# Key norms by squares and summed products instead of by the gram's diagonal, and the decay made at the head pair's own slot

## The reference, cut to what matters

```python
q, k, v = jnp.split(silu(causal_depthwise_conv(proj[..., :3072], conv_w)), 3, axis=-1)
k = t * lax.rsqrt(jnp.sum(t * t, axis=-1, keepdims=True) + RMS_EPS)      # t = k, per head; q likewise
g = -jnp.exp(a_log) * softplus(a + dt_bias)
gc = jnp.cumsum(g in chunks of 64)
decay = jnp.exp(jnp.where(causal, gc[..., :, None] - gc[..., None, :], -jnp.inf))
lower = jnp.where(strict, (k_beta @ k.T) * decay, 0)                     # solved as (lower + eye) x = rhs
attn = (q @ k.T) * decay
# scan over the 8 chunks, state carried along
v_new = u_c - w_c @ state
o_c = q_c @ state + a_c @ v_new
state = state * g_last + k_c.T @ v_new
```

## Time and profile before

| | before |
|---|---|
| median of 3 runs | 1973.99 us (1973.04 to 1975.83) |
| the profiled execution | 1975.83 us, its span 1974.0 us |
| granted TensorE clock, mean | 0.998 |
| PE busy | 1942.9 us, 98% of the span |
| DVE busy | 1161.7 us, 59% |
| ACT busy | 828.9 us, 42% |
| POOL busy | 28.6 us, 1% |
| chain that ended last | PE 86%, DVE 7%, ACT 4%, issue 2% |

### The profile page before, as it was taken

One profiled execution on the slowest core, in us unless ns is written; L12 is line 12 of the kernel. 1 busy time (PEld: TensorE's weight loads), 2 busy tenths in 40 slices (PEclk: granted clock), 3 DMA queues, 4 the chain that ended last, 5 costly groups with the idle time before them and its releaser, 6 DMA issues.

```text
span 1974.0 us, 28498 instructions
## 1 busy us (share of the span) xinstructions
PE 1942.9 (98%) x11058; PEld 1592.2 (81%) x11058; DVE 1161.7 (59%) x1899; ACT 828.9 (42%) x1347; POOL 28.6 (1%) x32
## 2 busy tenths in 40 slices
PE   9999999999999999999999999999999899999998
PEld 7776788888888787888888888778878678888887
DVE  6556477634556766667543654878887656424533
ACT  5456554333334444454333333545564632212232
POOL 0111000000000000000000000100000000000000
PEclk9999999999999999999999999999999999999999
DMA  6222122233223111122223224111211122232221
GB/s 217 76 75 96 43 80 92 89 103 106 86 80 112 70 65 65 65 86 86 101 87 111 91 76 142 64 50 50 70 44 44 65 86 91 101 107 86 105 87 64
DMA packets 30795, 168.40 MB, mean 85 GB/s; under 512 B 6456, under 2 KB 6616, under 8 KB 14816
## 3 DMA queue, kind: packets, MB, share of 16 engines
q1 hardware_dynamic: 25872, 161.69, 23.4%
q10 hardware_dynamic: 4816, 5.22, 0.8%
HBM read 163.72 MB, written 2.13 MB: 84 GB/s over the span
## 4 chain that ended last, share of the span: by engine, by line
PE 86%; DVE 7%; ACT 4%; issue 2%; DMA 0%; SPq 0%; DVEq 0%; ACTq 0%
PE bank L509 25%; PE bank L511 24%; PE bank L510 24%; PE bank L1148 2%; PE bank L792 1%; ACT hH L1337 1%; DVE hL L2152 1%; PE bank L975 1%; ACT wH L1337 1%; DVE x L2148 1%; PE bank L815 1%; PE bank L999 1%; PE bank L804 1%; PE bank L1226 1%; PE bank L1208 1%
## 5 line engine op out<-in xcount | busy, mean ns | idle before, releaser
L509 PE MATMUL bank<-hH,wH 128*128 128x512 f32 x1368 | 550.5, 402 | 1.7 <-DVE hL L2114 1.7
L511 PE MATMUL bank<-hH,wL 128*128 128x512 f32 x1368 | 532.6, 389 | 0.0
L510 PE MATMUL bank<-hL,wH 128*128 128x512 f32 x1368 | 531.7, 389 | 0.0
L1337 ACT ACTIVATE wH<-raw 128x2048 fp32r<-128x2048 f32 (+3 forms) x199 | 294.2, 1489 | 119.2 <-PE bank L511 104.8
L509 PEld LDWEIGHTS bank<-hH,wH 128*128 128x128 f32 x1368 | 257.6, 188 | 60.4 <-issue 8.4
L511 PEld LDWEIGHTS bank<-hH,wL 128*128 128x128 f32 x1368 | 257.1, 188 | 54.6
L2066 DVE TENSOR_TENSOR wL<-raw,wH 128x2048 fp32r<-128x2048 f32 x96 | 219.7, 2289 | 134.6 <-ACT wH L1337 134.6
L510 PEld LDWEIGHTS bank<-hL,wH 128*128 128x128 f32 x1368 | 257.8, 188 | 48.0 <-issue 1.2
L509 PE MATMUL bank<-mH,wH 128*128 128x512 f32 (+1 forms) x610 | 232.8, 382 | 0.0
L511 PE MATMUL bank<-mH,wL 128*128 128x512 f32 (+1 forms) x610 | 232.6, 381 | 0.0
L510 PE MATMUL bank<-mL,wH 128*128 128x512 f32 (+1 forms) x610 | 232.6, 381 | 0.0
(11 more groups left out here) (354 smaller groups left out, 2796.1 us busy)
## 6 DMA issues: line engine op xcount, KB each, us to landing
raw<-in_ffn_up SPq DMA_DIRECT2D x44, 1024.0 KB, 4.8
raw<-in_mlp_up SPq DMA_DIRECT2D x16, 1024.0 KB, 4.7
raw<-in_mlp_down SPq DMA_DIRECT2D x16, 1024.0 KB, 4.8
raw<-in_ffn_down SPq DMA_DIRECT2D x16, 768.0 KB, 4.1
raw<-in_odd_in SPq DMA_DIRECT2D x12, 1024.0 KB, 4.7
raw<-in_dn_qkv SPq DMA_DIRECT2D x12, 1024.0 KB, 4.8
raw<-in_ffn_down SPq DMA_DIRECT2D x16, 640.0 KB, 3.9
raw<-in_even_in SPq DMA_DIRECT2D x7, 1024.0 KB, 5.1
```

What stands on the lines that cost most here:

```text
L509: mm(out, a, c, start=first, stop=False, skip_group_check=joined)
L510: mm(out, a, d, start=False, stop=False, skip_group_check=joined)
L511: return mm(out, b, c, start=False, stop=last, skip_group_check=joined)
L1337: return nc.scalar.activation(out, in_, func, **kw)
```

## The change

- `key_sums` on VectorE goes. For pairs 1 to 3 ScalarE squares the keys at slot 48p-14 and TensorE sums them at slot 48p-12 with `squares_summed` into bank 4; `key_norm` moves to slot 48p-11 (was 48p-8), `key_base` to 48p-11 (was 48p-7), `key_exponents` to 48p-9 (was 48p-6).
- the gram of keys by keys of pairs 1 to 3 moves from slot 48p-10 and bank 4 to slot 48p and bank 3, ahead of the gram with the queries.
- the decay's exponent and Exp of pairs 1 to 3 move from slots 48p-6 and 48p-5 to 48p and 48p+1; the block from `lt` to the first transpose moves from 48p+1 to 48p+2.
- two of the preloads of the LOG_EXP set go, at the softplus of the gates and at `key_norm`.
- the turned gate rows are 64 instead of 32 (the cumulated gates and their Exps), turned at slot 10 (was 7), in bank 6 (was 7), and copied at VectorE's slot 7 (was 8); they are stored at ScalarE's slot 13 (was 10).
- `o_squared` waits for other events, since the buffer `sq` is used in another order.

```diff
-        rowsG, gl, gcB = sb("rowsG", [32, P]), sb("gl", [P, H, 8]), sb("gcB", [P, SEQ])
+        rowsG, gl, gcB = sb("rowsG", [64, P]), sb("gl", [P, H, 8]), sb("gcB", [P, SEQ])
-        key_size, tot = tok[:, 0, :], tok[:, 3, :]
+        key_size, gc_egc, tot = tok[:, 0, :], tok[:, 1:3, :].rearrange("p a b -> p (a b)"), tok[:, 3, :]
@@ TensorE
-                if t == 7:
-                    pe.wait_ge(*at("dn.gc_copied"))
-                    pe.wait_ge(*at("dn.lnss0"))
-                    nc.tensor.transpose(bank[7][0:32, 0:P], tok[:, 1, :], ident).then_inc(*tick("dn_gate_pe", "dn.rows_turned"))
+                if t == 10:
+                    pe.wait_ge(*at("dn.egc"))
+                    nc.tensor.transpose(bank[6][0:64, P:2 * P], gc_egc, ident).then_inc(*tick("dn_gate_pe", "dn.rows_turned"))
             def key_scalars(p, t):
-                if p and t == 38:
+                if p and t == 36:
                     pe.wait_ge(*at(f"dn.bv{p - 1}.1"))
-                    pe.wait_ge(*at(f"dn.silu{6 * p + 1}"))
-                    grams(p, 4, 0, f"dn.kk{p}")
+                    squares_summed("k", p, bank[4][:, 0:8])
...
-                                mm(bank[2][part(e), chunk(n)], ident[0:32, n:n + 1].to_broadcast([32, 64]), rowsG[:, part(e)],
+                                mm(bank[2][part(e), chunk(n)], ident[0:64, n:n + 1].to_broadcast([64, 64]), rowsG[0:64, part(e)],
...
-                        grams(p, 3, 0, f"dn.kk{p}")
                     else:
                         pe.wait_ge(*at(f"dn.y{p - 1}.5"))
+                    grams(p, 3, 0, f"dn.kk{p}")
+                    if p:
                         pe.wait_ge(*at(f"dn.silu{6 * p + 3}"))
                         grams(p, 2, 1, f"dn.qk{p}")
@@ ScalarE
-                a(lnss[:, p, :], lnss[:, p, :] if p else bank[7][:, 0:8], ACT.Ln, bias=eps)\
+                a(lnss[:, p, :], bank[4][:, 0:8] if p else bank[7][:, 0:8], ACT.Ln, bias=eps)\
...
                 a(gates_abs, gates_raw, ACT.Abs).then_inc(*tick("dn_gate_act", "dn.abs"))
-                nc.scalar.preload_act_table_set(LOG_EXP)
                 a(coef, v("a_log", 0, 8), ACT.Exp)
...
-                if t == (-5 if p else 1):
+                if t == 1:
                     act.wait_ge(*at(f"dn.din{p}"))
                     a(dec[:], dec[:], ACT.Exp).then_inc(*tick("dn_prep_act", f"dn.dec{p}"))
-                if t == 1:
                     squares_of("q", p, 1, f"dn.ksum{p}", *([f"dn.os{p - 2}.1"] if p >= 2 else []))
...
-                act.wait_ge(*at(f"dn.os2.{f}" if p == 3 else f"dn.qsum{p + 1}"))
+                act.wait_ge(*at(f"dn.os2.{f}" if p == 3 else f"dn.qsum{p + 1}" if f == 0 else f"dn.ksum{p + 2}" if p < 2 else "dn.qsum3"))
...
-                if t == 10:
+                if t == 13:
                     gate_rows_out()
...
-                    if t == 48 * p - 8:
-                        nc.scalar.preload_act_table_set(LOG_EXP)
+                    if t == 48 * p - 14:
+                        squares_of("k", p, 0, f"dn.qsum{p - 1}", *([f"dn.os{p - 2}.0"] if p >= 2 else []))
+                    if t == 48 * p - 11:
                         key_norm(p)
-                    if t == 48 * p - 6:
+                    if t == 48 * p - 9:
                         key_exponents(p)
@@ VectorE
-                if t == 8:
+                if t == 7:
                     dve.wait_ge(*at("dn.rows_turned"))
-                    nc.vector.tensor_copy(rowsG[:], bank[7][0:32, 0:P]).then_inc(*tick("dn_gate_dve", "dn.rows"))
-            def key_sums(p):
-                dve.wait_ge(*at(f"dn.kk{p}"))
-                dve.wait_ge(*at(f"dn.qsum{p - 1}"))
-                if p >= 2:
-                    dve.wait_ge(*at(f"dn.os{p - 2}.0"))
-                chain(tt(blocks(sq[:, 0, :]), blocks(bank[4][:]), over_chunks(eye), ALU.mult), "dn_scalar_dve", f"dn.diag{p}")
-                nc.vector.tensor_reduce(lnss[:, p, :], blocks(sq[:, 0, :]), AX.X, ALU.add).then_inc(*tick("dn_scalar_dve", f"dn.ksum{p}"))
+                    nc.vector.tensor_copy(rowsG[:], bank[6][0:64, P:2 * P]).then_inc(*tick("dn_gate_dve", "dn.rows"))
...
-                if t == (-6 if p else 0):
+                if t == 0:
                     dve.wait_ge(*at(f"dn.masked{p}" if p else "dn.spread0"))
...
-                if t == (1 if p else 2):
+                if t == 2:
                     dve.wait_ge(*at(f"dn.kk{p}"))
                     dve.wait_ge(*at(f"dn.dec{p}"))
-                    chain(tt(lt[:], bank[4 if p else 3][:], dec[:], ALU.mult), "dn_prep_dve", f"dn.lt{p}")
+                    chain(tt(lt[:], bank[3][:], dec[:], ALU.mult), "dn_prep_dve", f"dn.lt{p}")
...
-                    if t == 48 * p - 9:
-                        key_sums(p)
-                    if t == 48 * p - 7:
+                    if t == 48 * p - 11:
                         key_base(p)
```

More of the change, by code:

```diff
@@ L1877, in gate_rows_out @@
                 act.wait_ge(*at("dn.rows"))
-                act.dma_start(dram["gc_rows"], rowsG[:]).then_inc(*tick("dn_rows_stored", "dn.rows_stored", 16))
+                act.dma_start(dram["gc_rows"], rowsG[0:32, :]).then_inc(*tick("dn_rows_stored", "dn.rows_stored", 16))
             def gate_rows_in(p):
```

## The result

The changed kernel takes 1983.9 us (median of 6 runs, 1982.18 to 1985.61), the kernel before 1973.7 us beside it. The ratio is 1.0051, with a 95% interval from 1.0039 to 1.0063: 10 us slower, outside the 0.2% that a measurement of this kernel can tell. The profiled execution took 1984.93 us, its span 1983.1 us against 1974.0.

A forecast was written before the change was run, and what follows sets the result against it. TensorE, busy 98% of the span, was taken as the bound. Pairs 2.9 + 4.3 + 4.3 and gates -0.4 gave +11.1 us on a 1973.99 median: 1985.1 us, range 1977 to 1991.

The forecast's parts named there:

- The prep block: VectorE's block from lt to the first transpose, at slot 48p+2, delays the next solve: +2.0 us a pair.
- the bound of 2.8: Upper bound in us for the prep block's cost per pair, if all of it shows; lower bound 0.
- Rival C: The prep block hides, VectorE skipping ahead because TensorE is late too: +5.1 us, 1979.1; chance 0.10.
- The opening: Scan opening of pair 2 (pair 3 the same): write 1.5 us later, about 0.3 comes back, +1.2 at slot 96.
- The sums on TensorE: Key sums as 32 matmul records on TensorE for pairs 1 to 3, never hidden: 1.1 us each, 3.3 together.
- The table loads: ScalarE without the named set: ten more loads, 1.28 us each, costing only where TensorE waits; drain left out.
- rival A: One table set serves Ln and Exp, so the load at slot 48p-9 goes: +8.4 us, 1982.4; chance 0.14.
- Gates: First pair's gate rows turned at slot 10, copied earlier, one more load: -0.4 us, between -2 and +1.
- Rival B: Not slower: scalars are ready before the scan opens, idle 5.0 us goes, block fits: -2.1 us, 1971.9; chance 0.18.
- Rival D: Longer gaps bring half clock, one stretch behind each pair's opening, adding 5.1 us: 1990.2; chance 0.10.
- The signs: Profile after: solve waits about 10.8 us on VectorE, write 6 to 7 on ScalarE, ten loads, 96 records more.

The follow-up runs named there:

- experiment 1: The kernel before run again with no edit, against itself: 1974.19 against 1974.2 us, ratio 1.000.
- Experiment 4: The changed kernel with the decay's part undone (exponent at 48p-6, Exp at 48p-5, block at 48p+1): 1979.91 us, ratio 1.003 to the kernel before.
- experiment 3: The kernel before with the decay's part alone (exponent at slot 48p, Exp at 48p+1, block at 48p+2): 1991.7 us, ratio 1.0087.
- Experiment 8: The changed kernel with VectorE's block moved from slot 48p+2 to 48p+4, behind the right side, for pairs 1 to 3: 1987.38 us, ratio 1.0065 to the kernel before.
- experiment 7: The changed kernel with the sixteen products summing the keys' squares done twice in pairs 1 to 3: 1985.14 us, ratio 1.005 to the kernel before.
- Experiment 6: The changed kernel with the LOG_EXP set loaded by name again at the softplus and at slot 48p-11: 1981.21 us, ratio 1.0032 to the kernel before.
- experiment 9: The kernel before with key sums, Ln, Exps and decay spread over the scan's opening, behind the right side and vBlk: 1970.66 us, ratio 0.9985.
- experiments 1 to 4: The runs of experiment 1, of the gates' part alone on the kernel before (1972.76 us), of experiment 3 and of Experiment 4.

## Why the prediction was right

**The sum.** 1985.1 us was forecast and 1983.9 measured; in the profiled executions +11.1 and +9.1 us. The forecast's own mechanism is the one that the trace shows. Of its excess of 2.0 us the three pairs make 2.05 (0.66 + 0.71 + 0.68 less than worked out); what else moved (+0.96, -1.54 and +0.65 in the table) nearly cancels, and that is luck: none of the three was in the sum, and experiment 1 shows the first two without any change.

**The prep block, +2.0 a pair.** It measured 1.8 (5.67 against 3.86 us), in the order that was written down: state update, block, tap, right side. Experiment 4 gives 4.5 us for the three by the times and 5.3 by the traces. But experiment 3 corrects the reasoning: the bound of 2.8 ("all of it shows") was not the upper one, for ScalarE's Exp can start the block late, and the clock can fall on top. Rival C's argument, that the second gram gives VectorE 1.1 us, was dismissed for two reasons. The first, that VectorE waits for ScalarE's decay, is wrong for the changed kernel: its Exp ends at 1412.29, and the block starts at 1413.40, right behind the state update and output. The second, that the state update is queued first, holds: VectorE stood idle for 3.27 us ahead of it. Experiment 8 removes the thought that putting the block behind the right side would be enough.

**The opening, +1.2 at slot 96.** Measured +0.95 (solve of slot 96, 2.19 less 1.24). The steps came as worked out: 0.41 us of wait for the square (0.35 forecast), the first write 1.7 us later (1.45 forecast), the solve of slot 90 0.87 (1.2), the write of slot 92 1.15 (1.5) with a wait of 1.89, all counted from slot 84. The profile puts the solve's wait (0.69) down to ScalarE's read copy in pair 2 and to VectorE in pair 3: in pair 2 the copy ended at 1400.30 and the right side at 1400.29, TensorE going at 1400.54. The two end together, as close as the prediction had said.

**The sums on TensorE, "in full", 1.1 each.** One such group takes 1.03 us from start to start. "In full" was too strict: experiment 7 shows that in pair 2 a second group hides altogether, so that the opening there is set by ScalarE and VectorE; pair 3 has the same opening, but no undisturbed trace of it. In pair 1 all but the block came to 0.5 us (0.9 forecast). What the change costs by its sums alone was not separated.

**The table loads.** Ten more, as forecast. Experiment 6's trace puts four of them at 2.9 us, for which the working for rival A had 2.7 (1.06 in each of pairs 2 and 3 against 1.1, and 0.74 at the gates against 0.5). Rival A itself is out: the Trainium skill (ScalarE: Activation LUTs, Table sets: the hidden batching unit) has Ln and Exp share one load. Experiment 6's trace agrees, where the set is named; the changed kernel's, without the name, shows two (1395.18 and 1397.71). Nor does it show the drain of about 1.38 us that the Trainium skill (ScalarE: Activation LUTs, What ACT_TABLE_LOAD costs) adds to a load: the read copy of 1399.57 ends at 1400.30, the load runs from 1400.33 to 1401.61, and the SiLU starts at 1401.62. So leaving the drain out of the sum was right.

**Gates, -0.4.** Measured -0.42, with the waits 0.2, 0.31 and 0.79 where 0.5, 0.8 and 0.55 were worked out. The sum was better than its parts.

**Rival B, not slower.** It was to be decided by whether ScalarE ends its Exps before TensorE's read of slot 88. It did not: the read started at 1397.86, the Exps ended at 1399.67, in the time of before at 1398.4, where 1398.6 was worked out. B's mechanism is real, but not in this change: by experiment 9 some 3 us of the opening's waits go when the work is put behind vBlk. The change put it ahead, with two more loads and a square.

**Rival D.** No half-clock stretch stands behind an opening in the changed kernel's trace. But the rival is not out for every execution: the traces of experiments 7 and 8 have one in the opening of pair 3 and of pair 2. The changed kernel's own six times went from 1982.18 us at a mean clock of 1.000 to 1985.61 at 0.997. The one at the gates of the earlier trace rows is absent too, which gives its trace 1.5 us; I had not counted on that, and experiment 1 shows that the place of this stretch changes from one execution to the next.

**The signs.** Line 1217 waits 9.4 us (10.8 forecast), line 1225 6.5 (6 to 7), line 1127 0.31 (0.8), with ten more loads and 96 more records, as forecast. Two signs were written down wrong. The long waits at the solve come four slots after the write of slot 48p+2, at 48p+6, not two. And under rival A six more loads would have stood in the trace, not eight, as experiment 6 shows.

## What to carry to other kernels

When each engine's list is written by hand, count what stands ahead of the one instruction that TensorE waits for, on every engine, from the last event that holds all of them; that replay, done with a dozen rows, gave +11.1 us for a change that measured +10.2. Judge parts of a change together: here one part alone cost 17.5 us and the whole 10. Alone, it had a table load more on ScalarE and a gram less on TensorE ahead of the block, and the longer wait came with more half clock; how the difference divides between these was not measured. And where an engine has no room between two waits, another order only chooses who waits; take work out of the stretch, or behind the copy that is awaited.

## What the runs showed of the hardware that was not expected

A wait of 2.86 us at one solve came with some 10 us at a granted clock of 0.50 in two of three pairs, and with 3.4 us in the third; work that nobody needs, put in ahead of it, made the kernel 6 us faster. The length of the wait alone does not decide it: behind waits of 1.89 us at the same opening, experiment 8's trace has a stretch of 3.4 us in pair 2 and the changed kernel's has none. Between executions of the kernel before, whose times went from 1972.8 to 1976.1 us, the mean granted clock went from 1.000 to 0.997: of the 24 runs beside experiments 1 to 4, the ten at 0.999 or 1.000 took 1972.8 to 1973.6 us, the fourteen at 0.998 or 0.997 took 1974.0 to 1976.1.
